# Keys and values among the first transposes, one attention part rounded by VectorE, and four up-weight halves loaded earlier, in a one-layer decoder kernel

## What is computed

```python
h = rmsnorm(x, norm_mix)                       # x: (1, 512, 1024)
u, q, k, v, gate_s, gate_a = split(h @ w_in)   # 512, 512, 128, 128, 1024, 1024 columns
z = gelu(s5_mixer(u, ...))                     # diagonal state-space scan, 32 groups of 16 channels
branch_s = (z @ w_glu_val) * sigmoid(z @ w_glu_gate)
branch_a = sliding_window_attention(rmsnorm_heads(q), rmsnorm_heads(k), v, sinks) @ w_attn_up
x = x + (sigmoid(gate_s) * branch_s + sigmoid(gate_a) * branch_a) @ w_out
h2 = rmsnorm(x, norm_ffn)
# top group of 4, top two experts in it, SwiGLU experts: up 1024 x 512, down 256 x 1024
x = x + sum_e gate_e * (silu(g_e) * u_e) @ w_down[e]          # 16 experts
```

## Time and profile before

| | us |
|---|---|
| median of 3 runs | 572.87 |
| lowest and highest | 571.64, 579.38 |
| the profiled execution | 576.4 |
| its span | 574.4 |
| TensorE busy in the span | 530.4 (92%) |
| mean granted TensorE clock | 0.972 of full speed |

### The profile page before, as it was taken

One profiled execution on the slowest core, in us unless ns is written; L12 is line 12 of the kernel. 1 busy time (PEld: TensorE's weight loads), 2 busy tenths in 40 slices (PEclk: granted clock), 3 DMA queues, 4 the chain that ended last, 5 costly groups with the idle time before them and its releaser, 6 DMA issues.

```text
span 574.4 us, 7494 instructions
## 1 busy us (share of the span) xinstructions
PE 530.4 (92%) x2634; PEld 425.7 (74%) x2634; DVE 387.5 (67%) x652; ACT 282.4 (49%) x460; POOL 168.9 (29%) x348
## 2 busy tenths in 40 slices
PE   1699899999999999999999999968999999997993
PEld 1589787887787787777888888957787877775662
DVE  3994486784984975866565733468988888775650
ACT  4615225445445446464233411234767777765741
POOL 2341136179096096000000000022222331332233
PEclk9999999999999999999999999967999999998997
DMA  8723620220220211013366838428999999997432
GB/s 304 140 76 100 193 74 1 74 73 1 75 74 2 73 56 33 24 56 110 93 183 220 304 136 317 178 103 327 407 392 340 318 342 304 344 304 227 125 40 36
DMA packets 62901, 94.47 MB, mean 164 GB/s; under 512 B 14182, under 2 KB 45958, under 8 KB 62864
## 3 DMA queue, kind: packets, MB, share of 16 engines
q1 hardware_dynamic: 56288, 80.84, 40.9%
q0 software_dynamic: 5184, 8.41, 6.6%
q10 hardware_dynamic: 1392, 4.74, 2.1%
HBM read 88.71 MB, written 12.58 MB: 176 GB/s over the span
## 4 chain that ended last, share of the span: by engine, by line
PE 76%; DMA 8%; DVE 8%; ACT 4%; issue 1%; POOL 0%; ACTq 0%; POOLq 0%; DVEq 0%
PE pj L1618 11%; PE pj L1619 10%; PE pj L1620 10%; DMA arena_back<-in_w_expert_down_dram 5%; PE pj L1968 4%; PE pj L1970 4%; PE pj L1969 4%; PE m L1989 4%; PE sc L1695 3%; PE tp L1954 2%; DVE split L414 1%; DMA arena_back<-in_norm_mix_dram 1%; PE sc L1694 1%; PE m L1618 1%; PE m L1620 1%
## 5 line engine op out<-in xcount | busy, mean ns | idle before, releaser
L1618 PE MATMUL pj<-h_high,split 128*128 128x512 f32 x192 | 78.1, 407 | 2.4 <-DVE h_low L1076 2.3
L1619 PE MATMUL pj<-h_low,split 128*128 128x512 f32 x192 | 76.0, 396 | 0.0
L1620 PE MATMUL pj<-h_high,split 128*128 128x512 f32 x192 | 75.7, 394 | 0.0
L1498 DVE TENSOR_TENSOR up_low<-arena_front,up_high 128x2048 fp32r<-128x2048 f32 x24 | 54.9, 2289 | 8.2 <-ACT up_high L910 8.2
L577 POOL TENSOR_TENSOR rstd<-ssq,half_col 128x1 f32<-128x1 f32 x8 | 6.4, 798 | 162.0 <-DVE ssq L1027 150.3
L1968 PE MATMUL pj<-up_high,xt_high 128*128 128x512 f32 x128 | 50.7, 396 | 0.9 <-DVE xt_low L1532 0.9
L1970 PE MATMUL pj<-up_high,xt_low 128*128 128x512 f32 x128 | 50.4, 393 | 0.0
L1969 PE MATMUL pj<-up_low,xt_high 128*128 128x512 f32 x128 | 50.3, 393 | 0.0
L910 ACT ACTIVATE up_high<-arena_front 128x2048 fp32r<-128x2048 f32 x24 | 46.1, 1924 | 8.0 <-PE pj L1970 7.1
L414 DVE TENSOR_TENSOR split<-arena_front,split 128x2048 fp32r<-128x2048 f32 (+1 forms) x21 | 45.0, 2142 | 5.6 <-ACT split L407 5.5
L1618 PEld LDWEIGHTS pj<-h_high,split 128*128 128x128 f32 x192 | 36.8, 192 | 13.3 <-issue 3.4
(11 more groups left out here) (337 smaller groups left out, 1321.3 us busy)
## 6 DMA issues: line engine op xcount, KB each, us to landing
arena_front<-in_w_expert_up_dram SPq DMA_DIRECT2D x24, 1024.0 KB, 24.4
arena_back<-in_w_expert_down_dram SPq DMA_DIRECT2D x16, 1024.0 KB, 26.1
arena_front<-in_w_in_dram SPq DMA_DIRECT2D x13, 1024.0 KB, 5.5
arena_back<-in_w_expert_up_dram SPq DMA_DIRECT2D x8, 1024.0 KB, 24.1
arena_front<-in_w_out_dram SPq DMA_DIRECT2D x4, 1024.0 KB, 5.0
arena_back<-in_x_dram SPq DMA_DIRECT2D x4, 512.0 KB, 5.0
arena_front<-in_w_ssm_glu_gate_dram SPq DMA_DIRECT2D x8, 256.0 KB, 2.9
arena_front<-in_w_ssm_glu_val_dram SPq DMA_DIRECT2D x8, 256.0 KB, 3.4
```

The lines of the kernel that those rows point to most:

```text
L1498: tt(up_low[i % NH][:], ring[i % NH], up_high[i % 3][:].bitcast(F32), ALU.subtract).then_inc(up_low_done, 1)
L1618: pe.matmul(dst, sh, mh, start=first and i == 0, stop=False)
L1619: pe.matmul(dst, sh, ml, start=False, stop=False)
L1620: ins = pe.matmul(dst, sl, mh, start=False, stop=last and i == len(terms) - 1)
```

## The change

It has these parts. (1) `norm_mix` is loaded as one row, first in ScalarE's queue, and TensorE spreads it to 128 rows in the banks `m0`, `m1` by two matmuls with ones; a tile is scaled in two halves of 512, each with its own signal. (2) The key/value piece becomes piece 0 and is issued before x's last tile; the transposed tiles use four banks (tp and sc); TensorE turns tiles 0 to 2, multiplies keys and values of tile 0, turns tile 3, multiplies those of tiles 1 to 3, then `u`. (3) Key/value variances move to before the copy of `prm` in VectorE's list; both query pieces are split, with the four key/value normalisations between them, before the query products. GpSimd does the four key/value powers before the rotations, the rotations of chunk 0 in one go, then the four query powers. (4) At the end of the gate loop part 1 is rounded by VectorE's copy instead of ScalarE, and the last gelu's Square and Tanh stand ahead of the last attention rows in ScalarE's list. (5) The h2 buffers move to those of y_out, so `u4` is free; half 4 is loaded there after output piece 1, and halves 5 to 7 when the output units are done, before SyncE waits for the h2 stores and the first gather.

```diff
-        for t in range(TT):
-            tp_order += [("h", t, f) for f in range(2)]
+        pj_order += [("qkv", j) for j in range(TT)]
         pj_order += [("u", c) for c in range(CT_)]
+        pj_order += [("qkv", j) for j in range(TT, 2 * TT)]
...
-        pieces = [("in", 0), ("in", 256), ("in", KV0), ("in", SSM_W), ("in", SSM_W + 256)] + \
+        pieces = [("in", KV0), ("in", 0), ("in", 256), ("in", SSM_W), ("in", SSM_W + 256)] + \
...
+        slots = [("pair", HALF * i) for i in range(4)] + [("u4", 0)] + \
+                [("ht", HALF * i) for i in range(4)] + [("ga", HALF), ("uz", 0), ("uz", HALF)]
...
+        h2 = y_out
...
+            for t in range(TT - 1):
+                load_rows(t)
             load_piece(0)
+            load_rows(TT - 1)
             load_piece(1)
...
                 load_piece(n)
+                if n == P_OUT + 1:
+                    load_half(4)
...
             piece_used(sp, P_OUT + 2)
+            for i in range(5, 8):
+                load_half(i)
             for t in range(TT):
                 sp.wait_ge(h2_stored[t], 16)
             sp.wait_ge(gathered[0], 16)
-            for i in range(4, 10):
+            for i in range(8, 10):
                 load_half(i)
...
+            for j in range(TT):
+                inverse_root(qrs[:, j, 0:KVH], qss[:, j, 0:KVH], KVH, qk_var, j + 1, qk_rstd)
             g.wait_ge(rot_done, 1)
-            first_rotations(0)
-            double_rotations(1, 8)
-            for j in range(2 * TT):
-                H = KVH if j < TT else HEADS
-                inverse_root(qrs[:, j, 0:H], qss[:, j, 0:H], H, qk_var, j + 1, qk_rstd)
-            double_rotations(8, CH // 2)
-            g.sem_inc(e_done, 1)
+            rotations(0)
+            for j in range(TT, 2 * TT):
+                inverse_root(qrs[:, j, 0:HEADS], qss[:, j, 0:HEADS], HEADS, qk_var, j + 1, qk_rstd)
...
+            act.dma_start(mix_gain, norm_mix[0:1, :]).then_inc(mix_gain_loaded, 16)
...
+            square_rows(0)
             act.wait_ge(rows_loaded, 16 * 3)
             act.activation(ldt[:, 1, :], ldt[:, 0, :], ACT.Exp).then_inc(prm_act, 1)
+            square_rows(1)
+            square_rows(2)
...
+            turned_high(0)
+            split_high(P_KV)
+            turned_high(1)
+            square_rows(3)
+            turned_high(2)
+            split_high(P_U)
+            turned_high(3)
+            for j in range(TT - 1):
+                qk_out(j)
...
+            qk_out(TT - 1)
+            split_high(P_U + 1)
...
+                if i == 2 * DC:
+                    gelu_parts(CT_ - 1)
...
-                    if a == NQ - 1:
-                        high_zy(1, av_done, NQ - KVH)
...
             def scale_tile(t):
                 v.wait_ge(rstd_done, t + 1)
-                stt(xn[:, t, :], x_in[:, t, :], rstd[:, t:t + 1], mix_gain, ALU.mult, ALU.mult).then_inc(xn_done, 1)
+                v.wait_ge(gain_full, 2)
+                for f in range(2):
+                    fs = slice(f * 512, (f + 1) * 512)
+                    stt(xn[:, t, fs], x_in[:, t, fs], rstd[:, t:t + 1], mb[f][:], ALU.mult, ALU.mult).then_inc(xn_done, 1)
...
+            scale_tile(0)
+            row_variance(1)
+            scale_tile(1)
+            row_variance(2)
+            turned_low(0)
+            scale_tile(2)
+            split_low(v, P_KV)
+            turned_low(1)
+            row_variance(3)
+            scale_tile(3)
+            turned_low(2)
+            turned_low(3)
+            split_low(v, P_U)
...
+            for j in range(TT):
+                qk_variance(j)
...
-            split_low(v, P_QKV + 1)
-            for j in range(2 * TT):
+            split_low(v, P_Q)
+            for j in range(TT):
+                qk_normalise(j)
+            split_low(v, P_Q + 1)
+            for j in range(TT, 2 * TT):
                 qk_variance(j)
...
                 if i == 2 * DC - 1:
                     split_low(v, P_M)
+                    v.wait_ge(pj_full, pj_order.index(("gate", i)) + 1)
+                    v.wait_ge(av_done, NQ - KVH)
+                    dst, src = zy_parts(h_high)[1]
+                    mark(v.tensor_copy(dst, src))
                     low_zy(0)
...
+            pe.wait_ge(const_ready, 3)
+            for t in range(TT - 1):
+                turn_tile(t)
+            keys_values(0)
+            turn_tile(TT - 1)
+            for j in range(1, TT):
+                keys_values(j)
             for c in range(CT_):
```

More of the change, by code:

```diff
@@ L167, in hybrid_layer @@
         xt_high, xt_low = rounded("xt_high", "raw", 2 * D, [P, DC, P]), rounded("xt_low", "raw", 3 * D, [P, DC, P])
-        h2 = [part("u4", D * i, D) for i in range(2)]
         y_out = [part("att", 1280 + D * i, D) for i in range(2)]
+        h2 = y_out
         actT = [part("att", 1280 + 2 * D + 256 * i, 256, k=2, n=P) for i in range(2)]
@@ L458, in _, with load_rows @@
         def _(sp):
-            for t in range(TT):
+            def load_rows(t):
                 sp.dma_start(x_in[:, t, :], x[0, t * P:(t + 1) * P, :]).then_inc(x_loaded[t], 16)
@@ L773, in high_zy, with gelu_parts @@
                 act.activation(dst, src, ACT.Copy).then_inc(zy_high, 1)
+            def gelu_parts(c):
+                act.wait_ge(yv_done, c + 1)
+                act.activation(tb[2], tb[1], ACT.Square).then_inc(z_sq, 1)
+                act.wait_ge(z_arg, c + 1)
+                act.activation(tb[2], tb[2], ACT.Tanh, scale=GELU_IN).then_inc(z_th, 1)
             for i in range(2 * DC + 1):
@@ L887, in _ @@
                 act.wait_ge(x2_done, 2 * (u + 1))
-                if u >= 4:
-                    act.wait_ge(sq_done, TT + u - 3)
-                act.activation(part("att", u % 4 * 512, 512), x2[:, t, hf * 512:(hf + 1) * 512], ACT.Square, scale=D ** -0.5,
+                if u >= 2:
+                    act.wait_ge(sq_done, TT + u - 1)
+                act.activation(part("att", u % 2 * 512, 512), x2[:, t, hf * 512:(hf + 1) * 512], ACT.Square, scale=D ** -0.5,
                                accum_out=ssq[:, TT * (1 + hf) + t:TT * (1 + hf) + t + 1]).then_inc(sq_done, 1)
@@ L934, in rows_out @@
                 b = e % 2
+                if e == 0:
+                    for t in range(TT):
+                        act.wait_ge(h2_stored[t], 16)
                 if 2 <= e < HALVED + 2:
@@ L1628, in _, with keys_values @@
             h_hl = (h_high, h_low)
-            for b in range(2):
-                pe.wait_ge(tp_free[b], TT)
+            def keys_values(j):
+                b = fill(pj_order, pj_free, ("qkv", j))
+                tok = slice(j * P, (j + 1) * P)
+                w = piece_w(P_KV, k=DC, n=256)
+                if j == 0:
+                    piece_ready(P_KV)
+                half = DC // 2
+                for f in range(2):
+                    pe.wait_ge(h_low_done, 2 * j + f + 1)
+                    ins = product(pj[b][:, 0:256], [(both(h_hl, k, tok), both(w, k, slice(None))) for k in range(f * half, (f + 1) * half)],
+                                  first=f == 0, last=f == 1)
+                ins.then_inc(pj_full, 1)
+            pe.wait_ge(const_ready, 3)
[5 more added lines that the diff above has]
+                keys_values(j)
             for c in range(CT_):
```

222 lines of the change are left out of this document (103 added, 119 removed).

## The result

The changed kernel takes 568.67 us on the median of 19 runs (566.51 to 574.34), the kernel before 572.87 beside it (19 runs, 569.38 to 579.38). The ratio is 0.9914 with a 95% interval of 0.9893 to 0.9934: it is faster, by 0.9%, which is 4 to 6 us. The forecast was 560.5 and its range ended at 567, so the gain is about a third of the 12.4 us forecast.

What follows compares the result with a forecast made beforehand. Bound: TensorE's list plus stretches where it is empty or starved. Gains 4.8 + 1.8 + 6.9 = 13.5 us give 562.9 from the profiled 576.4, 559.4 from the median 572.87; weighted two thirds to the latter, 560.5; range 554.5 to 567.

Steps and rivals of the forecast that it cites:

- Queries start at 59.3: Front: the first query product waits for VectorE and starts at 59.3 us, 5.2 us earlier than before.
- 23.9 + 1.5: Front: VectorE's list before the queries takes 23.9 us without a gap, plus 1.5 us for contention with GpSimd.
- The far bound of 4 us: Front: most that VectorE could lose to GpSimd on the shared SBUF port, against 1.5 us taken.
- The gate loop starts 4.8 us earlier: Front's net gain at the gate loop: 5.2 us at the queries, less 0.4 for two key/value transposes among them.
- a lower clock after 25 us: Sign that would show the forecast wrong: TensorE at its lower clock after 25 us.
- the fourth rival: Front: the clock stays low through keys, values and `u`, 22 us more than forecast, total 582; chance 0.04.
- 1.8 us: Gate loop's end: the 1.3 us wait ahead of the merge goes, and 0.5 of the 0.8 us one.
- 7.4 us: Experts: the early halves remove all waits for loads and the low clock after them, a 7.4 us gain.
- 0.5 us: Routing: cost of the first gather meeting the tail of halves 5 to 7; bounds 0 and 3.5 us.
- a gather over 6 us from issue to landing: Sign that would show the forecast wrong, at the first gather of expert rows.
- 6.9: Experts: net gain in us of the early halves, 7.4 less 0.5; bounds 2 and 8.
- the third rival: Gather lands 3.5 us later, 2 us of expert waits stay; 6.9 becomes 1.4, total 566; chance 0.18.

Runs made afterwards that it cites:

- front_only: The changed kernel with the gate loop's end and the up-weight halves put back, leaving the front alone; 573.29 us, ratio 1.000 to the kernel before.
- halves_back: The changed kernel with halves 4 to 9 issued behind the first gather again; 568.76 us, ratio 0.9934 to the kernel before.
- split_back: The changed kernel with the second query piece split before the key/value normalisations and halves 4 to 9 behind the first gather; ratio 0.9831 to the kernel before.
- tail_only: The kernel before with the new end of the gate loop alone; 572.08 us, ratio 0.9951.
- after_store: The changed kernel with halves 5 to 7 issued once the h2 stores have landed; 568.15 us, ratio 0.9913 to the kernel before.
- halves_only: The kernel before with the four early halves alone, including the moved h2 buffers; 571.34 us, ratio 0.9983.
- filled_wait: The changed kernel with 16 matmuls, whose result nothing reads, ahead of TensorE's wait for the query weights' low part; ratio 0.9863 to the kernel before.
- scale_first: The changed kernel with the second query piece split before the normalisations and tile 0 scaled ahead of the `log_dt` rows; 566.02 us, ratio 0.9822 to the kernel before.

## Why the prediction was wrong, step by step

**"Queries start at 59.3": right.** 59.78 and 59.56 in two executions, with VectorE as the releaser. That it was met so closely is luck: errors in the terms cancelled. VectorE's list began at 35.10 instead of 33.9 (and the forecast's own terms, 30.8 + 0.6 + 1.9, make 33.3), since the `log_dt` load and the late rise of the clock delayed the key/value copies; and beside GpSimd the list took 24.5 us against 23.9 + 1.5. At most about 0.6 us went to contention, not 1.5: the query splits took 2304 ns beside the rotations, the weight splits 2289. The far bound of 4 us does not show. The timelines of VectorE and GpSimd tell why: it was GpSimd that stood still. Its product of 128x60 elements that begins just after VectorE's query split takes 2.41 us, as long as the split; one of 128x124 later takes 0.45.

```profile
57.34 2.29 DVE L411 TENSOR_TENSOR q_split<-arena_front,q_split 128x2048 fp32r<-128x2048 f32 x1
57.39 2.41 POOL L645 TENSOR_TENSOR arena_back<-arena_back 128x60 f32<-128x60 f32 x1
...
62.86 0.45 POOL L645 TENSOR_TENSOR arena_back<-arena_back 128x124 f32<-128x124 f32 x1
```

The Trainium skill, "SBUF — State Buffer", section "SBUF: two separate sides", says that whichever of the two engines starts first holds the shared port for its whole instruction and the other waits. This trace agrees: the long instructions are VectorE's, so the long waits fell to GpSimd, whose rotations were not on the path. The forecast had taken the rule for a loss of VectorE alone. The groups of VectorE from 24 to 97 us, after:

```profile
L411 DVE TENSOR_TENSOR split<-arena_front,split 128x2048 fp32r<-128x2048 f32 x3 | 6.9, 2289 | 0.3
L411 DVE TENSOR_TENSOR q_split<-arena_front,q_split 128x2048 fp32r<-128x2048 f32 x2 | 4.6, 2304 | 0.2
```

**"The gate loop starts 4.8 us earlier": failed.** It started 2.6 earlier. The step added the 2.8 us wait to the path and nothing behind it, but the wait, 3.8 us long, was followed by 3.4 us at the lower clock, which cost 1.6 us (the sign "a lower clock after 25 us", here at 60.6). The rows had it: the 3.6 us wait of the earlier trace rows has the clock of 0.86 behind it in the third step of the earlier trace rows, and the prediction counted that low clock among what would go. The clock was weighed only as a question for the whole front (the fourth rival), not as the price of the one wait that was itself forecast. With VectorE's split ahead of the normalisations the wait is 0.8 us and no lower clock follows it.

**"1.8 us" at the gate loop's end: right in kind, 1.0 to 1.4 in size.** The 1.3 us wait is gone; of the 0.8 us at the weight split 0.6 stays. front_only adds what the forecast had not seen: under the new front the same wait would have grown to 2.9 us.

**"7.4 us" of expert waits: one execution taken for the kernel.** The waits did go. Their size in five executions with the halves behind the gather is the length from the first down product to the last expert, less the 144.2 without waits: 7.4 before, 5.2 in halves_back, 5.1 in split_back, 4.5 in tail_only and 1.6 in front_only, 4.8 on the mean. The profile that gave the cost was the far one. The prediction noted that such waits were a likely place for its 3.5 us above the median, and then took the full 7.4 from the median as well.

**"0.5 us" back at the gather: the step that failed most.** It was 2.8 us by the first turned rows, 4.1 by the first down product in the two profiled executions (TensorE stands idle longer, and 4.8 us more of lower clock lie in it). Between the mean of the seven profiled executions with three halves there and that of the five with none, 35.1 and 31.3 us from the routing to the first down product, it is 3.8. The forecast set a store of 2.7 us at twice its time and took it to be hidden; it took 7.7, and its own landing is what the gather is issued on. The three loads were put at 8 us together; the last landed 13.3 us after the first was issued (369.31 to 382.6). The sign that was to warn of it, a gather over 6 us from issue to landing, did not come: the gather took 4.5 us, and the delay sat in the store ahead of it. By the turns between queues that the Trainium skill describes in "DMA: Bandwidth & Descriptors", section "Queues, rings and completion order", the forecast had put the store at twice its time. The runs show 2.9 times for the store; for the gather in after_store, 1.7 times, they agree. Net: 4.8 - 3.8 = 1.0 us for 6.9, which is what halves_only (0.9983) and halves_back against the changed kernel (0.9934, 0.9914) show. This was the third rival, "the early halves only move the wait": its price of 3.5 us at the gather was right, its 2 us of expert waits that stay were not there.

**The sum.** In place of 4.8 + 1.8 + 6.9 = 13.5 the traces give 2.6 + 1.4 + 1.0 = 5.0, the medians 4.2. The clock runs through what was missed. From 25 us to the merge the three profiles with the old front have 2.3 us at the lower level on the mean, the thirteen with the new front 7.3; where TensorE is busy throughout, 5 us more of it cost 2.5. The mean clock over the runs points the same way, 0.9729 before (27 runs) and 0.9675 after (19), but part of that difference is low clock that the record before leaves out.

**What stays open.** What sets the stretches of lower clock that appear in the gate loop of some executions (0 to 13.7 us of them there), where TensorE hardly waits. Over the 27 runs of the kernel before, mean clock and span go together (correlation -0.77). The kernels with the new front have more of them: 3.4 us or less from 25 us to the merge in the three profiles with the old front, 6.8 or more in ten of the thirteen with the new one. No run separates the order of TensorE's work from other causes. It was not tried either whether a first query product still earlier, at the pace of VectorE's list alone, would give more.

## What to carry to other kernels

Price a forecast wait of TensorE with what follows it: a wait of 3.8 us ahead of dense products cost 1.5 to 2.8 us more in lower clock, so moving one 2.3 us instruction of another engine off that wait gave more than its length (3.4 us by the medians, 0.8% by the ratios). That the whole kernel keeps all of such a gain is not shown. Before loads are moved ahead of a latency-bound step, count the megabytes in flight when that step's small transfers are issued; one megabyte made a 2.6 us store last 3.3 and cost nothing at the gather, three made it last 7.7. Take the size of a wait for loads from several executions. Before mean clocks are compared, look where the record of the clock begins: here two equal times had means 0.006 apart, which is as large as the difference between the kernels.

## What the runs showed of the hardware

- Among dense products the granted clock went down for 3.4 us, or 6.8 or 10.2, and the products of 512 columns then started 0.43 us apart. It happened at the end of an idle stretch of 3.8 or 3.9 us of TensorE in all five profiled executions that had one (the changed kernel twice, halves_back, after_store, front_only), and at the same place in none of the eight where that stretch was 0.2 to 0.9 us.
- It happens too where TensorE has not paused: in filled_wait it was busy 17.10 of 17.10 us, and the clock fell at the end of them.
- In the thirteen profiles with the new front the products began between 15.9 and 17.6 us and the clock rose to stay between 19.5 and 23.0, not in the order of their starts (15.9 and 20.8 in scale_first, 16.7 and 19.5 in front_only, 17.3 and 23.0 in the changed kernel).
- A store of 512 KB took 2.6 us, and 7.7 behind three loads of 1 MB issued up to 3.5 us ahead on another queue; a gather of 512 KB took 4.5 us, and 7.8 behind such loads.
- A GpSimd product of 128x28 or 128x60 elements that began within a VectorE split of 2.3 us took 2.3 or 2.4 us; one of 128x124 beside no VectorE instruction took 0.45.
